# Two transformer blocks on one core: the memory turned before the last inverse transform, named PSUM banks in the MoEs, and last products turned in halves

## The reference, cut to what matters

```
h  = rms(x);  p = h @ w_in
a  = MLA attention of p, 8 heads            # softmax(q k) v, low-rank q and k, v
z  = v; for n in 0, 1: z = gate[n] * (irfft(rfft(z) * kf[n]) + skip[n] * z)   # Hyena
x += [rms(a), rms(z)] @ w_out
x += cross attention of rms(x) on rms(mem)  # mem: 256 tokens, keys and values rms(mem) @ w_mkv
x += MoE(rms(x))                            # 32 experts, 2 per token
mod = silu(c) @ w_ada + b_ada               # 6 x 1024, shifts, scales and gates of block 2
u  = modulate(x);  lru = RG-LRU(conv(u)) * gelu(y);  att = attention(q, k, v) + rel_bias
x  = layernorm(a x + g1 * ([rms(lru), rms(att)] @ w_out2))
x  = layernorm(a x + g2 * MoE(modulate(x)))
```

## Time and profile before

| | |
|---|---|
| median of 3 runs | 1034.42 us (1033.56 to 1035.21) |
| profiled execution | 1035.14 us, its span 1033.1 us |
| mean granted PE clock | 0.988 of full |
| busy: PE, DVE, ACT, POOL | 986.1 (95%), 583.6 (56%), 352.2 (34%), 21.1 us (2%) |
| DMA | 289.04 MB, mean 280 GB/s |
| chain that ended last | PE 82%, DVE 9%, ACT 3%, DMA 3%, issue 2% |

### The profile page before, as it was taken

How to read it: one execution, slowest core, us unless ns; L and a number is a source line. 1 busy time by engine, 2 the same in 40 slices (tenths; PEclk the granted TensorE clock), 3 DMA queues, 4 the chain that set the end, 5 groups by cost and what they waited for, 6 DMA issues and landing times.

```text
span 1033.1 us, 14969 instructions
## 1 busy us (share of the span) xinstructions
PE 986.1 (95%) x5320; PEld 593.7 (57%) x5320; DVE 583.6 (56%) x1110; ACT 352.2 (34%) x679; POOL 21.1 (2%) x41
## 2 busy tenths in 40 slices
PE   8999999999999899999999999999899999999985
PEld 7678566977967533443443479876763434434434
DVE  5834437555345546445445475678675655555556
ACT  5654324455445222222222354754441111111113
POOL 1000001000000000000000000000000000000000
PEclk9999999999999899999999999989999999999998
DMA  9263492446407499999999927350619999999931
GB/s 360 120 250 137 195 397 102 163 183 243 166 1 319 180 362 427 424 425 424 428 423 429 397 83 324 141 228 1 245 62 385 423 427 424 426 424 426 424 153 41
DMA packets 28895, 289.04 MB, mean 280 GB/s; under 512 B 3080, under 2 KB 5544, under 8 KB 7728
## 3 DMA queue, kind: packets, MB, share of 16 engines
q1 hardware_dynamic: 25344, 282.04, 66.4%
q0 software_dynamic: 1136, 3.74, 1.1%
q10 hardware_dynamic: 2368, 2.64, 0.8%
HBM read 287.34 MB, written 1.06 MB: 279 GB/s over the span
## 4 chain that ended last, share of the span: by engine, by line
PE 82%; DVE 9%; ACT 3%; DMA 3%; issue 2%; DVEq 0%; SPq 0%; POOL 0%; ACTq 0%; POOLq 0%
PE bank L997 23%; PE bank L1011 11%; PE bank L627 7%; PE bank L628 6%; PE bank L629 6%; PE bank L1017 6%; PE bank L1004 4%; DVE ring_r L484 2%; PE bank L720 2%; PE bank L752 2%; PE bank L972 1%; PE bank L733 1%; PE bank L604 1%; DMA ring<-in_lat 1%; DMA HT<-in_rel_bias 1%
## 5 line engine op out<-in xcount | busy, mean ns | idle before, releaser
L997 PE MATMUL bank<-ring,arena 128*64 128x512 f32 x1040 | 237.5, 598 | 0.2 <-DVE arena L2218 0.2
L2248 DVE TENSOR_REDUCE arena<-bank 128x512 f32 x130 | 83.7, 686 | 117.3 <-PE bank L1017 114.8
L484 DVE TENSOR_TENSOR ring_r<-ring,ring_r 128x1024 fp32r<-128x1024 f32 (+1 forms) x84 | 99.2, 1211 | 85.1 <-ACT ring_r L477 85.1
L997 PEld LDWEIGHTS bank<-ring,arena 128*64 128x64 f32 x1040 | 69.1, 136 | 122.7 <-issue 122.7
L1011 PE MATMUL bank<-ring,arena 128*64 128x512 f32 x520 | 125.8, 604 | 0.5 <-DVE arena L2263 0.3
L477 ACT ACTIVATE ring_r<-ring 128x1024 fp32r<-128x1024 f32 (+1 forms) x84 | 84.8, 1046 | 78.8 <-PE bank L629 77.2
L627 PE MATMUL bank<-HT_r,ring_r 128*128 128x256 f32 x352 | 101.2, 288 | 5.4 <-issue 2.1
L629 PE MATMUL bank<-HT_r,ring_r 128*128 128x256 f32 x352 | 99.6, 283 | 0.0
L1590 ACT ACTIVATE arena<-bank 128x512 f32<-128x512 f32 x64 | 38.3, 598 | 147.6 <-PE bank L997 147.6
L1017 PEld LDWEIGHTS bank<-tab,arena 128*128 128x128 f32 x520 | 55.7, 140 | 54.8 <-issue 49.6
L1017 PE MATMUL bank<-tab,arena 128*128 128x128 f32 x520 | 70.9, 279 | 3.3 <-DVE arena L2277 2.1
(11 more groups left out here) (436 smaller groups left out, 1431.5 us busy)
## 6 DMA issues: line engine op xcount, KB each, us to landing
ring<-in_experts SPq DMA_DIRECT2D x64, 2048.0 KB, 14.8
ring<-in_experts SPq DMA_DIRECT2D x64, 1024.0 KB, 11.1
ring<-in_ada SPq DMA_DIRECT2D x12, 2048.0 KB, 10.1
ring<-in_win SPq DMA_DIRECT2D x5, 2048.0 KB, 11.4
ring<-in_hy SPq DMA_DIRECT2D x3, 2048.0 KB, 19.5
ring<-in_mk SPq DMA_DIRECT2D x2, 2048.0 KB, 11.1
ring<-in_mv SPq DMA_DIRECT2D x2, 2048.0 KB, 10.5
ring<-in_wo SPq DMA_DIRECT2D x2, 2048.0 KB, 7.3
```

The lines of the kernel that those rows point to most:

```text
L484: nc.vector.tensor_tensor(R(w), w, R(h), ALU.subtract).then_inc(sem("w_low"), 1)
L997: last = mm(gu_bank[g:g + WIN, :], xw[:, k, :], w[:, k * 512:(k + 1) * 512], start=k < 2, stop=k >= KD - 2)
L2248: last = V.reduce_sum(ysT[:, 4 * u:4 * u + 4, bass.ds(s, WIN)], dT_bank[u][:, :].rearrange("p (c g w) -> p c w g", c=4, g=2), AXX)
```

## The change

It moves work within each engine's sequence and renames banks:

1. MLA: `ada(3)` stands after `convolve(0)` and not at the head of head 2; its column product, evacuation and modulation follow in head 3. One product nobody reads is put inside `ada_col(1)`, and one each in heads 6 and 7.
2. The memory is loaded in head 0 to a place of its own, squared by ACT in heads 3 and 4 and normed by DVE in head 5; memT stands ahead of `convolve(1)`, DVE's low part ahead of `gated(1)`, and the five `occupy` products ahead of mk are gone.
3. The MoEs' stages name their banks. The gathers of the first three banks take token tile 0 as soon as its `sel` is there. In MoE 1, `bias` stands after swT. Numbers of `occupy` products change; in MoE 2, `gate_row` stands ahead of cnt.
4. At the end of a MoE the last `down_T` waits for each half of its input by itself; `scatter` waits for each half of the columns by itself.
5. `lss` is formed whole in head 1, after `wp_lru(0, 0)`; head 0 gets two `occupy` products.

```diff
-STAGES += [("cv1", 2), ("memT", 4), ("mk", 4), ...
+STAGES += [("memT", 4), ("cv1", 2), ("mk", 4), ...
+EXPERT = {1: (5, 6, 7, 0), 2: (4, 5, 6, 7)}
+SUMS = {1: (1, 2, 3, 4), 2: (0, 1, 2, 3)}
...
+        + [(f"swT{b}", 2, ((3, 4), (6, 7))[b - 1])] + [("bias", 1, (0,))] * one \
...
                         last = mm(ps[:, 4 * a + c:4 * a + c + 1], ada_sum(n)[:, c * P:(c + 1) * P], ones[:, 0:1],
                                   start=True, stop=True)
+                    if a + 1 < len(parts):
+                        mm(ps[:, 256:512], ident, T("iota")[:, 0:256], start=True, stop=True)
...
             for h in range(H1):
-                if h < 6:
+                if h < 6 and h != 2:
                     ada(h + 1)
+                if h == 3:
+                    ada_col(3)
...
+                if h >= 6:
+                    occupy(f"pv{h}", 0, 1)
                 ready(pe, f"pT{h}")
...
                 if h == 2:
                     convolve(0)
+                    ada(3)
                 if h == 5:
                     z_spectrum(1)
+            transposed("memT", mem, KD, "xn_m")
             convolve(1)
-
-            transposed("memT", XN, KD, "xn_m")
-            occupy("mk", 0, 5)
-            channel_out("mk", ["mk0", "mk1"], HT, low_m, banks_of("memT"))
+            channel_out("mk", ["mk0", "mk1"], HT, low_x, banks_of("memT"))
...
-                if b == 1:
-                    pe.wait_ge(sem("onehot"), 32)
-                    pe.wait_ge(sem("mask_row"), 1)
-                    ps = take(pe, "bias")
-                    full(mm(ps[0:H1, :], relb[0:BUCKETS + 1, :], oneh[0:BUCKETS + 1, :], start=True, stop=True), "bias")
...
+                occupy(f"gx{b}", 0, 6)
+                def gather(k, t):
...
+                gx = [take(pe, f"gx{b}", k) for k in range(3)]
+                for t in range(TT):
+                    pe.wait_ge(sem(f"sel{b}"), t + 1)
+                    pe.wait_ge(sem("xn_low"), TT * (b - 1) + t + 1)
+                    for k in range(3):
+                        gather(k, t)
...
+                if b == 1:
+                    pe.wait_ge(sem("onehot"), 32)
+                    pe.wait_ge(sem("mask_row"), 1)
+                    ps = take(pe, "bias")
+                    full(mm(ps[0:H1, :], relb[0:BUCKETS + 1, :], oneh[0:BUCKETS + 1, :], start=True, stop=True), "bias")
+                occupy(f"yTa{b}", 0, 2 if b == 2 else 1)
...
                 pe.wait_ge(sem(f"d_lo{b}"), NE)
+                pe.wait_ge(sem(f"y_out{b}"), NE - 1)
+                down_T(range(4))
                 pe.wait_ge(sem(f"d_hi{b}"), NE)
-                pe.wait_ge(sem(f"y_out{b}"), NE - 1)
-                down_T().then_inc(sem(f"yT_done{b}"), 1)
+                down_T(range(4, KD)).then_inc(sem(f"yT_done{b}"), 1)
...
+                    end = pt == NPAIR // P - 1
+                    for q in range(4):
+                        t, half = (q // 2, q % 2) if end else (q % 2, q // 2)
                         ready(pe, stage, 2 * (pt % 2) + half)
...
                 if h == 0:
-                    pe.wait_ge(sem("squared"), 4)
-                    lss = take(pe, "lss")
-                    token_sums(lss, sq, range(4), (0,))
-                    wp_ps["lss"] = lss
+                    occupy("ap0", 0, 2)
                 elif h == 1:
-                    full(token_sums(wp_ps["lss"], sq, range(4), (1,)), "lss")
                     pe.wait_ge(sem("lo_low"), 1)
                     wp_lru(0, 0)
+                    pe.wait_ge(sem("squared"), 4)
+                    full(token_sums(take(pe, "lss"), sq, range(4)), "lss")
...
+                if h == 0:
+                    act.wait_ge(sem("product"), TT)
+                    act.dma_start(mem, A["mem"].rearrange("(t p) d -> p t d", p=P)).then_inc(sem("mem_in"), 16)
+                if h in (3, 4):
+                    act.wait_ge(sem("mem_in"), 16)
+                    act.wait_ge(sem("zed"), TT)
+                    square(junk_m, three(mem[:, h - 3, :], 2), ssq_m[:, h - 3:h - 2])
             high(act, "mk0", (0, 1))
-            act.wait_ge(sem("mem_in"), 16)
-            squares("m", lambda t: XN[:, t, :], lambda t: junk_m, ssq_m, lambda t: None)
...
+                    normalised("m", lambda t: mem[:, t, :], lambda t: mem[:, t, :], rstd_m, "xn_m")
                     spectrum_product(1)
-            normalised("m", lambda t: XN[:, t, :], lambda t: XN[:, t, :], rstd_m, "xn_m")
             low(dve, "mk0", (0, 1))
+            low_evac("memT", HT, low_x, 4, lambda k: C("mem_norm_g", k))
             gated(1)
             dve.wait_ge(sem("zed"), 2 * TT)
-            low_evac("memT", HT, low_m, 4, lambda k: C("mem_norm_g", k))
```

More of the change, by code:

```diff
@@ L1013, in down, with down_T @@
                     return last
-                def down_T():
-                    for c in range(KD):
+                def down_T(chunks=range(KD)):
+                    for c in chunks:
                         last = tr(dT_bank[c // 4][:, (c % 4) * P:(c % 4 + 1) * P], d_sb[:, c * P:(c + 1) * P], ident)
@@ L1042, in step @@
                                 ready(pe, f"swT{b}", j)
+                            if b == 1:
+                                ready(pe, "bias")
                         before = 16 * (NE // RING) * (b - 1)
@@ L1097, in moe @@
                         down(w).then_inc(sem(f"extra_down{b}"), 1)
+                        if b == 2:
+                            pe.wait_ge(sem(f"extra_d{b}"), 2 * j + 1)
+                            down_T(range(4))
                         pe.wait_ge(sem(f"extra_d{b}"), 2 * j + 2)
-                        down_T().then_inc(sem(f"extra_yT{b}"), 1)
+                        down_T(range(4 if b == 2 else 0, KD)).then_inc(sem(f"extra_yT{b}"), 1)
                 start_sum((0, 1))
@@ L1116, in scatter @@
                     stage = (f"yTa{b}", f"yTb{b}")[pt // 2]
-                    for half in range(2):
+                    end = pt == NPAIR // P - 1
+                    for q in range(4):
+                        t, half = (q // 2, q % 2) if end else (q % 2, q // 2)
                         ready(pe, stage, 2 * (pt % 2) + half)
-                    for t in range(TT):
-                        for half in range(2):
-                            tok, cols = slice(t * P, (t + 1) * P), slice(half * 512, (half + 1) * 512)
-                            mm(acc[2 * t + half][:, :], R(swT[:, pt, tok]), R(ytok[:, pt, cols]), start=False, stop=False)
-                            last = mm(acc[2 * t + half][:, :], R(swT[:, pt, tok]), R(ytok_low[:, pt, cols]),
-                                      start=False, stop=pt == NPAIR // P - 1)
-                            if pt == NPAIR // P - 1:
-                                full(last, f"sct{b}", 2 * t + half)
+                        tok, cols = slice(t * P, (t + 1) * P), slice(half * 512, (half + 1) * 512)
+                        mm(acc[2 * t + half][:, :], R(swT[:, pt, tok]), R(ytok[:, pt, cols]), start=False, stop=False)
+                        last = mm(acc[2 * t + half][:, :], R(swT[:, pt, tok]), R(ytok_low[:, pt, cols]),
+                                  start=False, stop=end)
+                        if end:
+                            full(last, f"sct{b}", 2 * t + half)
                 pairs_T(f"yTa{b}", range(0, 4))
@@ L1434, in _ @@
             for h in range(H1):
-                if h < 6:
+                if h == 3:
+                    ada_evac(3)
+                if h < 6 and h != 2:
                     ada_evac(h + 1)
@@ L1548, in moe @@
                 A_(R(xn_high[:, 1, :]), XN[:, 1, :], ACT.Copy).then_inc(sem("xn_high"), 1)
+                if b == 2:
+                    for k in range(KD):
+                        last = A_(diag2[:, k, :], ident, ACT.Copy, scale=mod[:, 40 + k:41 + k])
+                    last.then_inc(sem("diag2"), 1)
                 act.wait_ge(sem("e_diff"), b)
@@ L1553, in moe @@
                 if b == 2:
-                    for k in range(KD):
-                        last = A_(diag2[:, k, :], ident, ACT.Copy, scale=mod[:, 40 + k:41 + k])
-                    last.then_inc(sem("diag2"), 1)
                     copies("g2r", [g2row[:, 0:512], g2row[:, 512:1024]])
-                if b == 1:
-                    ps = got(act, "bias")
-                    free(A_(brow[0:H1, :], ps[0:H1, :], ACT.Copy), "bias")
-                    ready(act, "bias")
-                    act.dma_start(bias_rows, brow[0:H1, :]).then_inc(sem("bias_out"), 16)
                 for k in range(0, KD, 2):
@@ L1575, in moe @@
                     last.then_inc(sem("x_high"), 1)
+                if b == 1:
+                    ps = got(act, "bias")
+                    free(A_(brow[0:H1, :], ps[0:H1, :], ACT.Copy), "bias")
+                    ready(act, "bias")
+                    act.dma_start(bias_rows, brow[0:H1, :]).then_inc(sem("bias_out"), 16)
                 for j in range(2):
@@ L2019, in _ @@
                 link(V.reciprocal(rinv[:, h, :], rsum[:, h, :]))
-                if h < 6:
```

(3 more changed lines are left out.)

49 lines of the change are left out of this document (23 added, 26 removed).

## The result

Four runs gave a median of 1016.82 us (1014.87 to 1018.58) against 1034.58 us before. The ratio is 0.9829 with a 95% interval of 0.9806 to 0.9852: 17.8 us faster, where 18.1 were forecast. The profiled execution is the quickest of the four, 1014.87 us with a span of 1012.9, so between the two profiles lie 20.2 us, not 17.8.

The account below looks back on a forecast made before the run. PE, busy 95% of the span, was taken to bound the kernel by its sequence, idle gaps and clock. Terms summed to -18.1 us: 1035.14 becomes 1017.0, the median 1034.42 becomes 1016.3; range 1013.2 to 1022.5.

Parts of the forecast that it names:

- The likeliest case: Whole kernel: all forecast terms hold, median 1016.3 us, own range 1014.8 to 1017.8, chance 0.41.
- the clock falls once, 1019.3: Rival: PE's clock falls at one of three sparse places, costing about 3 us, giving 1019.3; chance 0.33.
- A: MLA head 2: moving ada(3) removes PE's wait for its load and the low clock after it, -3.3 us.
- B: MLA, second inverse transform: memory prepared earlier, so mk starts with the transform's end, -3.1 us.
- The rule against it: MLA, second transform: behind transposes, which don't count as busy, it would start at the low clock.
- The rival of ACT blocked by the memory: MLA, head 3 and on: ACT waits up to 10 us for the memory's load, giving 1027; chance 0.04.
- C: MoE 1's prologue: early gathers and moved bias leave DVE setting the end; first expert at 351.35, -5.8 us.
- D: End of MoE 1: scatter(0) starts after one low part, not two; split transposes help too, -1.1 us.
- G: End of MoE 2: half of each down_T moves into a wait and scatter(0) starts earlier, -1.9 us.
- E: Block 2's attention, lss: the 0.71 us wait goes and the clock stays up, -2.9 us.
- F: MoE 2's prologue: gathers start some 1.3 us earlier, but the first expert waits for DVE, 0 us.

Follow-up runs that it names:

- A alone: Kernel before with only ada(3) moved behind the first inverse transform, its later steps in head 3, one unread product in ada_col(1): 1034.25 us, ratio 0.9990.
- kernel with whole ends: Changed kernel with whole down_T at the MoEs' ends and the scatter's waits and order as before; named banks stay: 1018.75 us, ratio 0.9844.
- kernel with new banks: Kernel before with only two block 2 stages in other PSUM banks (ak in 1 and 2, g1r in 3 and 4): 1027.78 us, ratio 0.9934.
- kernel with bias back: Changed kernel with MoE 1's bias product ahead of the gathers again; named banks and early gathers stay: 1018.63 us, ratio 0.9841.

## Why the prediction was right, and where it was not

**The sum.** 1016.3 was forecast and 1016.82 measured. Two errors of opposite sign lie in that. The sum lacked the bank choice of block 2 (2.1 us), and it took the clock as steady, while in four of nine executions of the changed kernel some 3 us go to the lower clock. The likeliest case and the rival "the clock falls once, 1019.3" are both true, of different executions: the lower group is near 1015.2, the upper one near 1018.3, and the median of few runs lies at either or between. That the median came within 0.5 us of the forecast is therefore luck; what the prediction had right is the terms. Where the clock falls in the upper group isn't shown, since both profiles of the changed kernel are of quick executions.

**A**, 2.8 for 3.3. The load is hidden as worked out. DVE's `mod` for `ada(3)`, which now stands in head 3 ahead of `pv`, makes PE wait 0.36 us; I had counted the moved products and not DVE's moved step behind them. That A gives nothing by itself is a thing the sum could not show: alone, in the one execution profiled, there were falls elsewhere.

**B**, 3.3 for 3.1, at its place. The rule against it, that transposes don't count as busy in the same way, so that the full clock doesn't engage for them (the Trainium skill, "TensorE: Matmul & The Clock Gate", Part 4: PE-mode transpose), did not decide: in ten profiles with the transposes between the heads and the transform, the transform starts at full clock each time, without unread products in two of them. The one profile with a fall there is of A alone, where the transposes still stand behind it. What the memory's load does to `ada3`, the prediction didn't price; together with A PE has no wait there, and alone it is 1.6 us of waiting (3.47 for 1.89). The rival of ACT blocked by the memory is out: the load lands in 4.8 us, and ACT has no wait for it.

**C**, 5.7 for 5.8. DVE's chain sets the end, 5.13 us from its memset to the first expert (340.18 to 345.31), and `bias` just fits, as worked out; PE waits for DVE's third copy, 0.74 us. By the comparison above, the gain is 2.3 us for the place of `bias`, with the fall that follows its wait, 1.7 for the bank of the turned weights and 1.6 for the clock. The prediction took the difference at DVE's chain in one piece and named neither of the last two.

**D and G**, 1.4 and 2.0 for 1.1 and 1.9: the `scatter` waits 0.39 us in place of 1.15, `down_T` no longer waits in one case and 0.80 us for 1.39 in the other. The kernel with whole ends gives back as much.

**E**, 3.1 for 2.9. Putting `lss` back costs that much by the medians. The gain is the clock's alone: in the kernel with new banks, where it holds, the old order takes 8.94 us for this stretch and the new one 9.08. The wait that went and the two unread products that came make a loss of 0.14 us together, where the prediction's 0.71 and 0.93 make one of 0.22. The clock at this place fell in six of the seven profiles with `lss` in two pieces, and in none of the seven with `lss` whole. Why it held in the kernel with new banks alone, with the same instructions and the same wait, stays open; filling the wait 30 us earlier doesn't do it, so PE's idleness there isn't the cause.

**The step that failed** is a term put at nothing without a reason: part 3 of the change speaks of the MoEs' banks alone, but the table also names those of block 2's stages, `ak` and `g1r` among them, and no term of the sum prices them. It measured 2.1 us. Before, `yl` takes a bank that `ak` holds; VectorE waits 1.42 us for ScalarE, makes two products of the LRU's gate and copies `ak` only at 656.48, and PE starts `yl` when its first copies are done, at 657.33. This wait of 1.88 us stood in the trace without a releaser. It goes with the new banks alone and comes back with the old ones. Any change of a bank table asks, for each stage, who had the bank before and when it is copied.

**F** was right: 0.0 us. The wait for DVE ahead of MoE 2's first expert grew from 0.21 to 0.78 us and 0.46 went into the turned weights, together 1.0 more where 1.3 were forecast.

## What to carry to other kernels

Read a change to a table of buffers stage by stage for who held each buffer before, also far from the place it was made for; a wait with no releaser in the profile is a candidate. Where the clock falls behind short waits and thin products, a gain of two microseconds is not additive: price edits in company, by profiles and mean clocks of single executions, and not only by medians. And put the small work that nobody waits for (column sums, a bias product) behind dense work, not into the gap it seemed to fill: for the column sums here that was worth 3 us where the clock fell, and nothing where it held.

## What the hardware showed unasked

The time lost to the lower clock comes in like portions: 1.7, 3.4 or 5.1 us, for 20 falls in ten of the 14 profiles. The falls at the end of each profile, behind PE's last product, are not counted. A window of one such fall, from the kernel with bias back:

```profile
116.00:122.00 6.00, 6.00 (x35) 2.94 (x36) 0.46 (x2) 1.24 (x4) 0.00 (x0) 0.72 0.97 360
```

The same instructions fall in one execution and not in another: at 116 to 122 us in two of eight profiles in which PE has the same program up to there. A load of 1 MB on ACT's queue landed in 4.8 us, where it took 12.8 in its old place. What differs is the traffic it met: in the changed kernel it is issued at 115.26, with the DMA engines nearly idle (share 0.03 from 114 to 116 us) and four loads of 2 MB following on SP's queue from 116.41 on; before, it is issued at 151.7 into a stretch with a share of 0.95 to 0.99. How two queues share the engines isn't shown by this.
